# Column quarters for the head combine of a hybrid decoder step on one Trainium2 core

## The reference

```python
def moba_attend(q, q_pos, k_sel, v_sel, idx, valid, k_own, v_own, own_start, slopes):
    ...
    s = jnp.concatenate([s_sel.reshape(B, H, Tq, n_sel), s_own], axis=-1)
    p = jax.nn.softmax(s, axis=-1).astype(v_own.dtype)
    o = (jnp.einsum('bhqjk,bhqjkd->bhqd', p[..., :n_sel]..., v_sel) + jnp.einsum('bhqk,bkhd->bhqd', p[..., n_sel:], v_own))
    return o.astype(q.dtype)

def trunk_layer(x, ...):
    z = rmsnorm(x, norm1_g) @ w_in
    q, k, v, u = jnp.split(z, [ATTN_WIDTH, 2 * ATTN_WIDTH, 3 * ATTN_WIDTH], axis=-1)
    a = attend(q, k, v)
    p, new_hist = pool_mixer(u, hist, start_pos, w_pool, pool_scale)
    x = x + jnp.concatenate([a, p], axis=-1) @ w_out
    h2 = rmsnorm(x, norm2_g)
    x = x + (jax.nn.silu(h2 @ w_gate) * (h2 @ w_up)) @ w_down
```

## Time and profile before

| what | value |
|---|---|
| median of three runs | 1491.95 us (1491.08, 1491.95, 1493.06) |
| the profiled execution | 1492.57 us, of which the span is 1490.8 us |
| PE busy, share | 1413.6 us, 95% |
| DVE / ACT busy | 888.2 / 503.5 us |
| mean granted clock of PE | 0.978 |
| HBM read and written | 328.10 MB, 5.27 MB |
| the combines' passes (line 1527) | 128 passes, 17.1 us busy |

### The profile page before, as it was taken

How to read it: one execution, slowest core, us unless ns; L and a number is a source line. 1 busy time by engine, 2 the same in 40 slices (tenths; PEclk the granted TensorE clock), 3 DMA queues, 4 the chain that set the end, 5 groups by cost and what they waited for, 6 DMA issues and landing times.

```text
span 1490.8 us, 34214 instructions
## 1 busy us (share of the span) xinstructions
PE 1413.6 (95%) x13918; PEld 1307.1 (88%) x13918; DVE 888.2 (60%) x1319; ACT 503.5 (34%) x666; POOL 108.9 (7%) x184
## 2 busy tenths in 40 slices
PE   6998999998788999999999999999999999999986
PEld 5987777766555789999999999999999999999986
DVE  4778777767666545765555554555464646464645
ACT  4422122112123333543343434333333333333333
POOL 2127500000001000210000000000000000000003
PEclk9999999999899999999999999999999999999998
DMA  5788999999999666655555555555555555555531
GB/s 181 265 327 284 368 400 401 401 398 392 397 366 324 198 208 210 193 162 170 165 164 165 169 166 164 164 168 168 163 164 167 168 163 163 167 169 163 163 125 64
DMA packets 164279, 334.40 MB, mean 224 GB/s; under 512 B 10223, under 2 KB 54440, under 8 KB 163599
## 3 DMA queue, kind: packets, MB, share of 16 engines
q1 hardware_dynamic: 164183, 333.06, 66.3%
HBM read 328.10 MB, written 5.27 MB: 224 GB/s over the span
## 4 chain that ended last, share of the span: by engine, by line
PE 81%; SPq 7%; DVE 5%; DMA 3%; issue 2%; ACT 1%; POOL 0%; POOLq 0%; ACTq 0%; DVEq 0%
PE banks L1398 24%; PE banks L1399 24%; PE banks L1400 23%; PE banks L1511 5%; SPq L420 2%; SPq L424 2%; DVE kpage L880 2%; PE banks L1404 2%; SPq L442 2%; PE banks L1493 2%; DMA vpage<-in_cache_v 1%; DMA kpage<-in_cache_k 1%; DMA w_raw<-in_w_out 1%; DMA vec<-in_pool_scale 1%; SPq L412 1%
## 5 line engine op out<-in xcount | busy, mean ns | idle before, releaser
L838 DVE TENSOR_TENSOR w_lo<-w_raw,w_hi 128x1024 fp32r<-128x1024 f32 x360 | 439.7, 1228 | 429.6 <-ACT w_hi L572 429.0
L1398 PE MATMUL banks<-hh,w_hi 128*128 128x288 f32 x2176 | 646.9, 297 | 4.6 <-DVE w_lo L838 1.5
L1399 PE MATMUL banks<-hl,w_hi 128*128 128x288 f32 x2176 | 645.2, 297 | 0.0
L1400 PE MATMUL banks<-hh,w_lo 128*128 128x288 f32 x2176 | 642.9, 295 | 0.5 <-issue 0.5
L572 ACT ACTIVATE w_hi<-w_raw 128x1024 fp32r<-128x1024 f32 x360 | 378.9, 1058 | 682.0 <-PE banks L1400 459.6
L1398 PEld LDWEIGHTS banks<-hh,w_hi 128*128 128x128 f32 x2176 | 411.2, 189 | 22.7 <-issue 19.0
L1399 PEld LDWEIGHTS banks<-hl,w_hi 128*128 128x128 f32 x2176 | 411.5, 189 | 1.1 <-issue 1.1
L1400 PEld LDWEIGHTS banks<-hh,w_lo 128*128 128x128 f32 x2176 | 410.5, 189 | 0.5 <-issue 0.5
L1398 PE MATMUL banks<-ah,w_hi 128*128 128x288 f32 x704 | 208.9, 297 | 9.5 <-DVE af L1254 5.4
L1400 PE MATMUL banks<-ah,w_lo 128*128 128x288 f32 x704 | 209.7, 298 | 0.0
L1399 PE MATMUL banks<-al,w_hi 128*128 128x288 f32 x704 | 209.4, 298 | 0.0
(11 more groups left out here) (193 smaller groups left out, 644.5 us busy)
## 6 DMA issues: line engine op xcount, KB each, us to landing
kpage<-in_cache_k SPq DMA_DIRECT2D x128, 512.0 KB, 7.8
vpage<-in_cache_v SPq DMA_DIRECT2D x128, 512.0 KB, 6.9
w_raw<-in_w_gate SPq DMA_DIRECT2D x88, 512.0 KB, 3.6
w_raw<-in_w_up SPq DMA_DIRECT2D x88, 512.0 KB, 3.6
w_raw<-in_w_down SPq DMA_DIRECT2D x88, 512.0 KB, 3.7
w_raw<-in_w_in SPq DMA_DIRECT2D x64, 512.0 KB, 9.5
w_raw<-in_w_out SPq DMA_DIRECT2D x32, 512.0 KB, 4.1
xs<-in_x_prompt SPq DMA_DIRECT2D x2, 1024.0 KB, 7.3
```

Source lines behind the costliest of these rows:

```text
L838: V.tensor_tensor(w_lo[:, s, :], w_raw[:, s, :], w_hi[:, u, :].bitcast(F32), ALU.subtract).then_inc(lo_ready, 1)
L1398: PE.matmul(o, wh, xh[:, c, :], start=start and i == 0, stop=False)
L1399: PE.matmul(o, wh, xl[:, c, :], start=False, stop=False)
L1400: last = PE.matmul(o, wl, xh[:, c, :], start=False, stop=stop and i == len(chunks) - 1)
```

## The change

The 8 matmuls of a combine no longer add up in one 32-partition region. Head h writes to the 32 columns of quarter h mod 4, so each quarter holds the sum of two heads, and bank 6 holds four quarters on 128 partitions. `o_all` has 128 partitions instead of 32, with the same bytes in each, and ACT copies 128x128. DVE copies `eo` to the four quarters of a new tile `eo4`, settles, and scales all 128 partitions. In place of the 8 transposes, PE multiplies each 128x128 block of o_all (as weights) with a 128x32 table `fold`, which has a one where the partition mod 32 is the column: it transposes and adds the four quarters. The table is part of the first load.

```diff
+        "fold": (p % 32)[:, None] == np.arange(32),
...
-        o_all = sb("o_all", [32, NB, DH], stack=mid)
+        o_all = sb("o_all", [P, NB, DH], stack=mid)
...
+        eo4 = sb("eo4", [P, NB], stack=post)
...
-                copy(o_all[:, b, :], OB[0][0:32, 0:DH]).then_inc(comb_saved, 1)
+                copy(o_all[:, b, :], OB[0][:, 0:DH]).then_inc(comb_saved, 1)
...
             lo_out(11)
+            for g in range(4):
+                own.did(V.tensor_copy(eo4[32 * g:32 * g + 32, :], eo[:, :]))
+            own.settle()
             dve.wait_ge(comb_saved, NB)
-            V.tensor_tensor(o_all[:, :, :], o_all[:, :, :], eo[:, :].unsqueeze(2).to_broadcast([32, NB, DH]),
+            V.tensor_tensor(o_all[:, :, :], o_all[:, :, :], eo4[:, :].unsqueeze(2).to_broadcast([P, NB, DH]),
                             ALU.mult).then_inc(own_scaled, 1)
...
                 for h in range(H):
-                    last = PE.matmul(OB[0][0:32, 0:DH], headsel[:, h, :], osb[:, DH * h:DH * h + DH],
-                                     start=h == 0, stop=h == H - 1)
+                    g = h % 4
+                    last = PE.matmul(OB[0][32 * g:32 * g + 32, 0:DH], headsel[:, h, :], osb[:, DH * h:DH * h + DH],
+                                     start=h < 4, stop=h >= 4)
                 last.then_inc(comb_done, 1)
...
             for b in range(NB):
-                last = turn(bank[7][:, 32 * b:32 * b + 32], o_all[:, b, :], 32)
+                last = PE.matmul(bank[7][:, 32 * b:32 * b + 32], o_all[:, b, :], tb("fold"), start=True, stop=True)
             last.then_inc(t1_in, 1)
```

## The result

The changed kernel's median is 1494.34 us (22 runs, 1491.20 to 1499.36) against 1491.03 us (22 runs, 1487.63 to 1493.80) for the kernel before, measured anew beside it: ratio 1.0023, 95% interval 1.0016 to 1.0030. It is slower by about 3.4 us. The forecast was 1492.0, 1489.3 to 1494.3, "same" most likely, with 3.0 us as the edge of "same"; the measured median lies just above that range. The forecast was reckoned from a median before of 1491.95; with the 1491.03 measured now its +0.1 gives 1491.1, so the true miss is about 3.2 us. The profiled execution took 1494.63 us with a span of 1492.1.

The account below looks back on a forecast made before the run. DMA transfers were taken to bound the early stretch, PE alone from 526.4 us on. Combine 7 -1.3, fold +1.29, DVE 0 and table +0.1 summed to +0.1 on a median of 1491.95: 1492.0 us, range 1489.3 to 1494.3.

Parts of the forecast that it names:

- Table and layout: First load: 32 more columns add 16 KB, 0.09 us at most; o_all keeps its bytes per partition; taken as +0.1 us.
- rival 2: Around 395 to 514: longer PE idles bring two more spells at 1.2 GHz, +3.4 us, giving 1495.4; chance 0.08.
- Combines 0 to 6 at nothing: Before 526 us: savings of 1.3 us each hide under transfers, DVE's chain or a late w_out tile; 0 on the path.
- Combine 7 at 0.56: On the unbroken PE chain at 543.94: quarters take 0.56 us instead of 1.86, saving 1.3 us.
- rival that quarters don't run side by side: In the combines: so short a group saves nothing, the fold still costs 1.29, giving 1493.3; chance 0.07.
- The fold at 1.90, +1.29: On PE's chain at 556.42: fold matmuls take 1.90 us where eight transposes took 0.61, so +1.29 us.
- rival that it costs as much as block-sum pairs: At the fold: it costs +3.2 us instead of +1.29, giving 1493.9; chance 0.04.
- DVE at 0.6 us under cover: Ahead of o_all's scaling: four copies and a settle take 0.6 us, hidden by 3.2 and 2.2 us of cover; cost 0.
- The waits of PE near 506 longer by up to 1.3 us: Expected sign: PE waits up to 1.3 us longer each for the DVE maximum and for ACT near 506.
- Sum without the layout: Whole kernel, instruction terms only: combine 7 at -1.3, fold at +1.29, DVE at 0.
- Rival 1: Full-DMA and mixed stretches: PE time counts after all; all seven earlier combines give 9.1 us, 1482.9, likelier 1487; chance 0.09.
- SP issuing its last K page more than 1 us earlier: In the page-load stretch: named as a sign that would show the forecast wrong.

Follow-up runs that it names:

- e6: Kernel before with 128 unused bytes per partition behind an unchanged table, so every later tile starts 128 bytes further; 1495.06 us against 1490.70, ratio 1.0027.
- e9: Kernel before with 128 unused bytes ahead of the V pages alone, K pages and w_raw as before modulo 256; 1495.31 us against 1490.12, ratio 1.0026.
- e1: Kernel before with the new table and tiles in place but none of the new instructions; 1494.73 us against 1490.03, ratio 1.0041.
- e3: Changed kernel's quarters in all eight combines, but closing part scales and transposes the first quarter only, against the kernel before; 1492.85 us against 1490.03, ratio 1.0019.
- e2: Changed kernel with the old one-quarter combines and a fold table zero past row 31, against the kernel before; 1496.44 us against 1490.03, ratio 1.0049.
- e5: Changed kernel with 128 unused bytes behind the table, restoring later starts modulo 256, against the kernel before; 1489.68 us against 1490.70, ratio 0.9990.
- e8: Kernel before with combine 7 alone in quarters, its block alone folded, and pads putting w_raw, K and V pages on 256-byte multiples; 1485.89 us against 1490.70.
- e12: Changed kernel with pads putting w_raw, K and V pages on multiples of 256 bytes, against the kernel before; 1485.63 us against 1490.12, ratio 0.9973.
- e7: Kernel before with three pads so w_raw, K and V pages all start on multiples of 256 bytes; 1482.83 us against 1490.70, ratio 0.9948.
- e11: Kernel before with w_raw alone moved from 32 to 160 bytes past a multiple of 256; 1487.83 us against 1490.12, ratio 0.9980.
- e13: Changed kernel with K and V pages on multiples of 256 bytes and w_raw at 160, against the kernel before; 1485.26 us against 1491.26, ratio 0.9963.

## Why the prediction was wrong

The step that failed is "Table and layout", which stood at +0.1 us. It priced 32 more table columns at 16 KB of load, +0.1 us, and looked at addresses only as bytes used ("the same bytes per partition as before"). They moved every tile by 128 bytes and the V pages off a multiple of 256, worth +4.4 to +5.2 us (e6, e9; e1, with the table, +4.7; about +4.0 for e6 and e9 by their ratios). The size fits the stretch by an estimate: the DMA engines are full from about 182 to 462 (shares of 0.98 to 1.05), and 6 of 399 GB/s less over 280 us is 4.2 us. The sum is not seen piece by piece in a trace: in the pair of profiles the late w_out tile comes at the same moment, and only over all sixteen does it come later at the lower rate. I had called that stretch bound by the loads and used it only as cover for PE's savings; a bound by loads is also the place where a loss of rate is paid in full.

The terms of the instructions were right to 0.2 us: -1.29 and +1.09 on the chain, where -1.3 and +1.29 were forecast. The number of rival 2, 1495.4, lay nearer to the measured 1494.34 than the forecast did; that is luck, since the reason it gave, shorter combines, is not the one that the runs show.

The rest by its own steps:
- Combines 0 to 6 at nothing: right as far as the runs can tell. e3, with all eight, is 1.9 us under e1, of which combine 7 is 1.3. SP's waits for PE in the changed kernel are 4.7 us in 192, before 4.0.
- Combine 7 at 0.56: 0.57 on the chain. The rival that quarters don't run side by side fell. The reading behind it had a slip: the V sums' 0.128 us a pass is less than the combine's 0.134, not "hardly more".
- The fold at 1.90, +1.29: 1.70 on the chain, +1.09; e2 against e1 says +1.7 us for fold and copies, within what six runs can tell. By the Trainium skill's factor of 4 ("TensorE: Matmul & The Clock Gate", its terms table) it would have been 2.44 us, an estimate from the page; the trace does not agree, it has 2.8 times the transposes. The rival that it costs as much as block-sum pairs (+3.2) fell.
- DVE at 0.6 us under cover: 0.73, and covered.
- The waits of PE near 506 longer by up to 1.3 us: 4.02 for 2.90, and 0.81 for the maximum.
- Sum without the layout: +0.0, and by the rows of the chain 1.09 - 1.29 = -0.2; e5 measured -1.0 (-2.8 to -0.1), the table's load included.
- Rival 1, the earlier combines counting after all: e3 against e1 leaves 0.6 us for seven of them, where 9.1 was the full price.
- Rival 2, the clock. The spells did lengthen in the changed kernel's profile (0.64 in 504.6:514.1), and there they took the 1.2 us shown above; that sign of being wrong came true. But e5 has the same instructions and is no slower than before, and e1 and e6 have none of them and lose the whole sum. So shorter combines are not the cause of the loss. The mean granted clock over all runs is 0.977 for the changed kernel, 0.979 for e1, e5 and e6 and 0.980 before; what share of the 3.4 us went by way of the clock stays open.

Another sign named in the prediction, SP issuing its last K page more than 1 us earlier, looked the wrong way: it came at 465.2 after 465.7. The rate in the forty slices shows what happened: 401 to 393.

## What to carry to other kernels

Where loads are the bound, a change that allocates anything ahead of a loaded tile can change its start modulo 256 bytes, and this may outweigh the instructions that were changed. So print the starts before and after; a pad costs only its bytes, and here three pads gave 7.9 us to a kernel in which no instruction was touched. When a whole effect is unexplained, time the new tables and tiles without the new instructions first: this one run took the fold, the copies and the quarters out of the question and left the table or the addresses.

## What the hardware showed unexpectedly

- Full-DMA rate by starts (182:374): K and V pages both on multiples of 256 bytes 403 to 408 GB/s (406 to 408 with w_raw on one too); V alone 398 to 400; neither 392 to 393. The share of busy DMA engines reads 1.04 in all of them, so busy share tells nothing of it.
- The FFN loop's pace on PE depends on placement by up to 0.5%: 6036 passes in 800 us with `hh` and `w_hi` at 96 and w_raw/w_lo at 0 modulo 256 (e8, e12), 6056 to 6058 before, in the changed kernel and in e7, 6064 and 6065 with 224 and 160 (e11, e13). Over the loop's 800 us that is about 4 us. Which tiles must not meet, and why, stays open: no run moved hh and w_hi alone.
- Four column quarters of 128x32 weights in fp32 take 0.57 us for 16 passes of 128 columns, against 1.86 in one quarter.
